# Token rows kept in PSUM through the expert blocks, and one weight load for the fullest expert's two blocks

## The reference, cut to what matters

```
gl = x2 @ w_rg + b_rg                        # 4 groups, the best is taken
el = x2 @ w_re + b_re                        # 8 experts in it, the best 2 are taken
w  = softmax(two logits) * p(group)
for each chosen (token, expert):             # 32 experts, 1024 -> 512 -> 1024
    y += w * ((silu(x @ w_gate[e]) * (x @ w_up[e])) @ w_down[e])
h  = h + y
out = rmsnorm(h) * final_norm_g
```

## Time and profile before

| | us |
|---|---|
| median of 3 runs (1507.97 to 1509.42) | 1508.8 |
| the profiled execution's own time | 1504.2 |
| its span, first to last instruction | 1502.6 |
| PE busy | 1150.9 (77%) |
| DVE busy | 464.5 (31%) |
| ACT busy | 234.5 (16%) |
| POOL busy | 207.2 (14%) |

### The profile page before, as it was taken

The page is one execution under the profiler, slowest core; times in us unless marked ns, Lnnn a source line. Parts: engine busy times, 40 slices in busy tenths (PEclk is TensorE's granted clock), DMA queues, the critical chain, the costliest instruction groups (busy, mean ns, idle before and its releaser), DMA issues. The chain is left out here.

```text
span 1502.6 us, 22749 instructions
## 1 busy us (share of the span) xinstructions
PE 1150.9 (77%) x7953; PEld 729.8 (49%) x7953; DVE 464.5 (31%) x1117; ACT 234.5 (16%) x646; POOL 207.2 (14%) x402
## 2 busy tenths in 40 slices
PE   5899999999995898877899999666565656565650
PEld 3666667666763455554566664443232333232320
DVE  2235654656455574333000001331111111111113
ACT  1132233223322353222000000000000000000000
POOL 3033433344324111010000000000000000000003
PEclk9799999999997998999899999678887888787875
DMA  6033424332422226542965360299999999999963
GB/s 197 20 113 88 115 84 143 104 99 84 143 59 56 51 49 175 133 148 84 255 155 134 80 232 0 77 413 426 429 428 428 428 427 429 429 427 428 428 283 123
DMA packets 171882, 315.69 MB, mean 210 GB/s; under 512 B 22162, under 2 KB 153810, under 8 KB 159170
## 3 DMA queue, kind: packets, MB, share of 16 engines
q1 hardware_dynamic: 161842, 303.34, 56.1%
q0 software_dynamic: 2048, 6.95, 1.6%
q10 hardware_dynamic: 7952, 4.88, 1.1%
HBM read 296.02 MB, written 19.11 MB: 210 GB/s over the span
## 5 line engine op out<-in xcount | busy, mean ns | idle before, releaser
L1696 PE MATMUL ph<-w_gate_up,x_gathered 128*32 128x256 f32 x1408 | 121.8, 521 | 108.7 <-DMA w_gate_up<-in_w_exp_up 108.1
L669 PE MATMUL psg<-stretch 128*128 128x336 f32 x512 | 159.8, 477 | 11.3 <-DVE h_sample_out L647 9.6
L1696 PEld LDWEIGHTS ph<-w_gate_up,x_gathered 128*32 128x32 f32 x1408 | 60.5, 148 | 170.1 <-issue 98.1
L669 PEld LDWEIGHTS psg<-stretch 128*128 128x128 f32 x512 | 103.7, 204 | 69.2 <-DVE h_sample_out L647 15.4
L1664 DVE SCALAR_TENSOR_TENSOR h_gate<-h_tanh,ph 128x128 f32<-128x128 f32 x33 | 9.5, 287 | 387.3 <-ACT h_tanh L1624 387.3
L1696 PE MATMUL ph<-stretch,x_gathered 128*32 128x256 f32 x704 | 60.7, 519 | 57.9 <-DMA stretch<-in_w_exp_up 57.9
L584 DVE SCALAR_TENSOR_TENSOR x_conv<-x_padded,conv_wh,x_conv 128x360 f32<-128x360 f32 x96 | 56.9, 593 | 101.0 <-ACT x_conv L533 90.0
L678 PE MATMUL psg<-stretch 128*128 128x256 f32 (+1 forms) x384 | 84.5, 380 | 0.0
L1346 PE MATMUL psm<-stretch,w_merge 128*128 128x336 f32 x256 | 75.8, 455 | 6.9 <-DMA w_merge<-in_w_in 6.9
L1745 POOL DMA_INDIRECT y_expert<-expert_rows,slot_i x6 | 5.7, 958 | 505.8 <-PEq L1715 504.2
L678 PEld LDWEIGHTS psg<-stretch 128*128 128x128 f32 (+1 forms) x384 | 67.3, 177 | 14.5
(11 more groups left out here) (415 smaller groups left out, 1659.4 us busy)
## 6 DMA issues: line engine op xcount, KB each, us to landing
w_down<-in_w_exp_down SPq DMA_DIRECT2D x33, 2048.0 KB, 40.4
w_gate_up<-in_w_exp_gate SPq DMA_DIRECT2D x22, 2048.0 KB, 33.8
w_gate_up<-in_w_exp_up SPq DMA_DIRECT2D x22, 2048.0 KB, 38.4
stretch<-in_w_exp_gate SPq DMA_DIRECT2D x11, 2048.0 KB, 34.1
stretch<-in_w_exp_up SPq DMA_DIRECT2D x11, 2048.0 KB, 38.7
stretch<-in_w_in SPq DMA_DIRECT2D x16, 1024.0 KB, 5.3
stretch<-in_w_in SPq DMA_DIRECT2D x16, 512.0 KB, 7.5
h<-in_state_ssm SPq DMA_DIRECT2D x16, 512.0 KB, 4.8
```

What stands on the lines that cost most here:

```text
L669: mm = pe.matmul(ps[m][:, 0:T], wg[:, k, P * m:P * m + P], S["xnT"][:, k, :], start=(k == 0), stop=(k == KT - 1))
L1696: mm = pe.matmul(ph[h][32 * j:32 * j + 32, 0:256], xg[h][:, k, :], w_gu[w][:, :, k, P * j:P * j + P], start=(k == 0), stop=(k == KT - 1))
```

## The change

- `xtok` is multiplied by the identity into six PSUM banks (`acc`) in the route phase, as the start of a sum that stays open. The six banks hold the 336 rows until the end; `ph`, `px` and `py` share the other two.
- The slots of the pairs and their weights are also laid out along the free axis on all partitions (`slot_row`, `weight_row`): 12 matmul calls, four ACT copies, two POOL and two DVE multiplications in the route phase.
- In each block DVE makes from them a matrix `back` (32 slots x 4 groups of partitions, 336 tokens: the weight where slot and token belong together; four more instructions). After `py` has been copied to `yr`, PE adds the block to `acc` by 12 calls. A call has 32 rows of `yr` (one group of partitions j, a quarter of the columns) against up to 128 tokens. DMAs to `ydram`, the buffer itself and its zeros are gone.
- The fullest expert (of 3 to 31) changes places with expert 28, so that it is block 28, and its rows 32 to 63 are block 31. Expert 31 is block 32. Block 31 loads nothing and uses the weights of block 28, which are still in buffer 1. Blocks over are counted from 33 (`NMAIN`) on. The expert of each block from 3 on is read from `blk_e`.
- `each_block`: a loop of 4 passes (blocks 0 to 23), blocks 24 to 32 written out, then the loop of 4 passes of six bodies under `If`. With the counts above all 24 of these are jumped over.
- The final phase is part of the moe phase: no gather and no sum, ACT squares `acc` once PE has closed it, and DVE scales from `acc` to `xtok`.

```diff
+NMAIN = NE + 1
+TWICE, AGAIN = 28, 31
-NBLK = NE + NOVER
+NBLK = NMAIN + NOVER
+ADD_ORDER = [(0, 0), (0, 1), (0, 2), (0, 3), (1, 0), (1, 1), (1, 2), (1, 3), (2, 0), (2, 2), (2, 1), (2, 3)]
@@ attention_phase
-            sp.dma_start(S["ydram"][NE * BLK:SLOTS, :].rearrange("(b p) d -> p b d", p=64),
...
-            v.memset(blank, 0.0)
@@ route_phase, gpsimd
+            pool.wait_ge(topw_ok, 1)
+            for j in range(2):
+                pool.tensor_tensor(dgw[:, j, :, :], bc(S["ident"][:, :].unsqueeze(1), [P, 3, P]),
+                                   bc(S["topw"][:, :, j:j + 1], [P, 3, P]), ALU.mult).then_inc(dgw_ok, 1)
@@ route_phase, scalar
+            for j in range(2):
+                act.wait_ge(row_ps, j + 1)
+                act.activation(S["slot_row"][:, j, :], ps[j][:, 128:128 + T], ACT.Copy).then_inc(row_ev, 1)
... (the same for weight_row)
@@ route_phase, tensor, ahead of and behind the nine matmuls
+            for j in range(4):
+                pe.matmul(acc[:, j, :], S["ident"][:, :], S["xtok"][:, 0:2, 256 * j:256 * j + 256],
+                          start=True, stop=False)
+            for i in range(2):
+                pe.matmul(acc[0:80, 4 + i, :], S["ident"][0:80, 0:80], S["xtok"][0:80, 2, 512 * i:512 * i + 512],
+                          start=True, stop=False)
...
+            for src, ok, freed in ((dgs, dgs_ok, 0), (dgw, dgw_ok, 2)):
+                for j in range(2):
+                    pe.wait_ge(ok, j + 1)
...
+                    for t, r in enumerate(ROWS):
+                        mm = pe.matmul(ps[j][:, 128 + COL[t]:128 + COL[t] + r], o[0:r, :], src[0:r, j, t, 0:r],
+                                       start=True, stop=True)
+                    mm.then_inc(row_ps, 1)
@@ route_phase, vector, behind the nine matmuls: 45 instructions in place of 23, from
+            v.scalar_tensor_tensor(key[:, :], cnt[:, :], 64.0, keyb[:, :], ALU.mult, ALU.add)
...
+            v.tensor_reduce(topn[:, 0:1], key[:, :], AX.X, ALU.max)
...
+            for j in range(2):
+                v.tensor_tensor(dgs[:, j, :, :], bc(S["ident"][:, :].unsqueeze(1), [P, 3, P]),
+                                bc(S["slot"][:, :, j:j + 1], [P, 3, P]), ALU.mult).then_inc(dgs_ok, 1)
@@ moe_phase, each_block
-            sure = NE // UNROLL
+            sure = TWICE // UNROLL
             with eng.Fori(0, sure) as i:
                 for u in range(UNROLL):
-                    body(UNROLL * i + u, u, i)
-            with eng.Fori(sure, -(-NBLK // UNROLL)) as i:
+                    body(UNROLL * i + u, u, 2 * i + loads(u))
+            for b in range(sure * UNROLL, NMAIN):
+                body(b, b, loads(b))
+            with eng.Fori(0, -(-NOVER // UNROLL)) as i:
                 for u in range(UNROLL):
-                    with eng.If(UNROLL * i + u < nblk):
-                        body(UNROLL * i + u, u, i)
+                    with eng.If(UNROLL * i + u + NMAIN < nblk):
+                        body(UNROLL * i + u + NMAIN, u + NMAIN, 2 * i + loads(u + NMAIN))
@@ moe_phase, sync
-            for b in range(3, NE):
+            with sp.Fori(1, 10) as i:
+                for u in range(3):
+                    load(3 * i + u, u, bass.ds(3 * i + u, 1))
+            for b in (30, 32):
+                load(b, b % 3, slice(b, b + 1))
@@ moe_phase, scalar
-                act.wait_ge(y_sent[h], 64 * (3 * i + u // 2) + 64)
-                act.activation(yr[h][:, :], py[h][:, 0:256], ACT.Copy).then_inc(y_ev, 1)
+                act.wait_ge(added, b + 1)
+                act.activation(yr[h][:, :], py[:, :], ACT.Copy).then_inc(y_ev, 1)
...
-                for j in range(4):
-                    act.dma_start(ydram[bass.ds(BLK * b, BLK), j, :], yr[h][32 * j:32 * j + 32, :]
...
+            act.wait_ge(all_added, 1)
+            for t in (2, 0, 1):
+                act.activation(as_tile(xsq[0:r, :], t), tile_rows(t), ACT.Square, ...
@@ moe_phase, vector
+            def weights_back(b, h):
+                v.scalar_tensor_tensor(weq[:, :, :], slot_row[:, :, :], lane[:, 0:1], weight_row[:, :, :],
+                                       ALU.is_equal, ALU.mult)
+                v.drain()
+                v.wait_ge(added, b + 1)
+                v.tensor_tensor(back[h][:, :], weq[:, 0, :], weq[:, 1, :], ALU.add).then_inc(back_ok, 1)
+                v.tensor_scalar(lane[:, :], lane[:, :], float(BLK), None, ALU.add)
@@ moe_phase, tensor, body: gate, up and gather as before, then
                 pe.wait_ge(ht_ok, b + 1)
+                pe.wait_ge(xt_ok, b + 2)
... (down)
+                pe.wait_ge(y_ev, b + 2)
+                pe.wait_ge(back_ok, b + 1)
+                for t, j in ADD_ORDER:
+                    r, q = ROWS[t], slice(32 * j, 32 * j + 32)
+                    if (t, j) == (2, 1):
+                        mm.then_inc(tail_half, 1)
+                        pe.wait_ge(tail_half, b + 1)
+                    mm = pe.matmul(token_rows(t, j), back[h][q, COL[t]:COL[t] + r], yr[h][q, :], start=False,
+                                   stop=False)
+                mm.then_inc(added, 1)
@@ moe_phase, tensor, at the end
+            for i in range(6):
+                r = P if i < 4 else 80
+                mm = pe.matmul(acc[0:r, i, 0:CLOSE], S["zeros"][:, 0:r], S["ident"][:, 0:CLOSE], start=False, stop=True)
+            mm.then_inc(all_added, 1)
-def final_phase(nc, A, S, sem):
...
```

More of the change, by code:

```diff
@@ L901, in _ @@
                     load_kv(2 * i + half, half, True)
-            sp.wait_ge(blank_out, 16)
         @block.gpsimd
@@ L1405, in route_phase @@
                                                                      "mask_ok", "rank_ps"))
+        topw_ok, dgw_ok, dgs_ok, row_ps, row_ev = (sem(n) for n in ("topw_ok", "weight_diag_ok", "slot_diag_ok",
+                                                                    "slot_row_ps", "slot_row_ev"))
+        acc = S["acc"]
         block = ctx.enter_context(nc.Block())
@@ L1515, in _ @@
+            v.tensor_copy(rank[0:80, 2, :], ps[0][0:80, 64:96])
+            v.drain()
+            v.tensor_scalar(most[:, :], key[:, :], topn[:, 0:1], None, ALU.is_equal)
+            v.tensor_reduce(nb[:, :], over[:, :, :], AX.X, ALU.add)
+            v.drain()
+            v.tensor_tensor(far2[:, :], most[:, :], over[:, :, 0], ALU.mult)
+            v.tensor_tensor(key[:, :], most[:, :], to28[:, :], ALU.mult)
             v.tensor_scalar(late[:, :, :], rank[:, :, :], BLK - 0.5, None, ALU.is_gt)
@@ L1575, in moe_phase @@
         yr = [tsb(f"y_block{h}", [P, 256]) for h in range(2)]
-        px, ph, py = ([ctx.enter_context(nc.psum_tensor(f"{n}{h}", [P, 512], F32)) for h in range(2)]
-                      for n in ("px", "ph", "py"))
+        lane, lane_b = tsb("lane", [P, 1]), tsb("lane_shift", [P, 4])
+        weq, back = tsb("weighted_eq", [P, 2, T]), [tsb(f"weights_back{h}", [P, T]) for h in range(2)]
+        fg, ss = tsb("final_g", [P, D]), tsb("ss3", [P, 4])
+        out = S["xtok"]
+        xsq = S["hn"][:, 0, :]
@@ L1671, in body @@
                 pick(h)
+                v.drain()
+                weights_back(b + 1, 1 - h)
             pick(0)
+            for j in range(3):
+                v.tensor_scalar(lane_b[:, j:j + 1], S["part_f"][:, 0:1], 32.0 * (j + 1) - 0.5, -float(BLK), ALU.is_gt,
+                                ALU.mult)
+            v.drain()
+            v.tensor_tensor(lane[:, :], lane_b[:, 0:1], lane_b[:, 1:2], ALU.add)
+            v.drain()
+            v.tensor_tensor(lane[:, :], lane[:, :], lane_b[:, 2:3], ALU.add)
+            v.drain()
+            v.tensor_tensor(lane[:, :], lane[:, :], S["part_f"][:, 0:1], ALU.add)
             gathered(1, 0)
             pick(1)
+            v.drain()
+            weights_back(0, 0)
             each_block(v, nblk, body)
+            v.wait_ge(g_in, 16)
+            for t, n in ((2, 1), (0, 3), (1, 3)):
+                r = ROWS[t]
+                v.wait_ge(ssq, 6 + n)
+                v.wait_ge(rs_ok, 6 + max(n - 1 + t % 2, 1))
+                v.scalar_tensor_tensor(as_tile(out[0:r, t, :], t), tile_rows(t), ss[0:r, t:t + 1],
+                                       as_tile(fg[0:r, :], t), ALU.mult, ALU.mult).then_inc(out_ok, 1)
         @block.tensor
```

262 lines of the change are left out of this document (142 added, 120 removed).

## The result

The changed kernel takes 1571.05 us (median of 4, 1568.52 to 1574.21), the kernel before 1508.38 (4 runs, 1506.86 to 1509.42): ratio 1.0417, 95% interval 1.0396 to 1.0439, so 4.2% slower. The profiled execution took 1570.66 with a span of 1569.0. The forecast was 1494.6. What came true is rival A (1561.6), and the time lies 5 us above the range.

What follows compares the result with a forecast made beforehand. It took moe to be bound by weight transfers (15.0 us an expert), with route, jumps and final uncovered. Terms -6.9 (up to the jumps), +11.9, -18.3, -0.9 sum to -14.2: 1494.6 us, own range 1484 to 1505, whole range 1485 to 1566.

Steps and rivals of the forecast that it cites:

- rival A: Loop of six bodies no longer stays in PE's instruction memory, later passes miss: +67 us, 1561.6; chance 0.35.
- The jumps: PE's jumps over never-run bodies after the last block: 27.5 us in place of 15.6, +12 us.
- B: Only the dropped instruction packet is fetched again, once a pass: +10.5 us, 1505; chance 0.10.
- The main loop: Loop over the main blocks: instruction misses there would lie hidden under the 14.7 us of a load.
- Route: Route phase before moe: more DVE instructions (+4.3) and slot and weight rows (+5.2), +9.5 us, bounds +8 and +15.
- D: Route costs more, ranks delayed and DVE at its old average: +5.5 us, 1500; chance 0.06.
- The stream: Weight transfers in moe: one load less (14.7 us) and no writes of `y` (10 us), -24.7 us.
- that hole: Start of moe, 998 to 1013 us: the DMA queue runs dry for a moment, 1.4 us lost.
- The last blocks: Blocks 30 to 32 run in a row on PE, block 32 starting 9.1 us after its weights: +8 us given back.
- C: Adds don't overlap between groups of partitions: 2.9 us more in each of the last three blocks, +9, 1503.5; chance 0.04.
- Final: From the closing matmuls to the end: 11.0 us in place of 29.3, gather and sum gone, -18.3 us.
- the attention term: Start of the attention phase, before route: DVE's memset of 0.91 us goes, -0.9 us.

Runs made afterwards that it cites:

- shift64: The changed kernel with 16 useless one-column matmuls (64 PE instructions) behind block 28, moving the loop over further blocks within its page: 1504.0 us, ratio 0.9960.
- straight: `guard` with the 33 main blocks written out one after the other on PE, ACT and DVE in place of a loop: 1474.7 us, ratio 0.9783.
- guard: The changed kernel with the whole loop over further blocks inside one If on every engine, one jump in place of 24: 1478.4 us, ratio 0.9802.
- early_pair: `straight` with the fullest expert's two blocks at 13 and 16 in place of 28 and 31: 1471.4 us, ratio 0.9751.
- reload: `guard` with a weight load put back for block 31 (expert 31's weights, as many bytes), undoing the saved load: 1485.6 us, ratio 0.9851.
- jump_hidden: `early_pair` with the jump over the further blocks ahead of block 32 instead of behind it: 1472.3 us, ratio 0.9759.
- short_bodies: The changed kernel with one add of twelve in the never-run bodies over, cutting that loop from 1797 to 1533 instructions: 1501.1 us, ratio 0.9950.

## Why the prediction was wrong, step by step

**The jumps** are the step that failed: "six jumps over bodies that never ran [...] and three passes of 2.65: 27.5". Measured 96.2, so 68.7 too little; rival A's term was 67. `shift64` shows the forecast's own number where the loop stays: its jumps last from 1463.4 to 1490.9, 27.5 us. So the step rested on one assumption, that the longer loop stays in PE's instruction memory, and the prediction gave it 0.45 against 0.35 with the count of pages (eight or nine) in hand and "that eight do is shown nowhere" written down. The Trainium skill ("Runtime: NRT & Kernel Launch", section "Instruction fetch mechanics") has the FIFO of 2048 instructions and the sequential fetch from which the ninth page follows; the ten loops and the nine packets a pass above agree with that part of the section, and this rule should have had the larger chance. Rival A was also put too simply: it "decides from the first packet too many", while with eight pages the place in the last page decides. Even a reader sure of A's mechanism would have needed the loop's address. B (one packet a pass) is excluded: nine packets came in a pass, and nearly every jump missed.

**The main loop:** "the same misses would lie under the 14.7 of a load" was right. Its branch back misses three times at 6.3 to 6.6 us, and writing the blocks out brought 3 to 4 us (`straight` against `guard`), which is within the intervals.

**Route:** +7.7 against +9.5. DVE's chain took 11.7 (982.45 to the end of 994.13), forecast 11.6. The multiplications into `acc` did delay the ranks (980.56 behind 978.84), but they took 0.30 to 0.39 a pair in place of 0.6, so they ended 10.0 after route's start and not 11.2. The granted clock over them was 1.00 (980.5 to 982.45 us), before 0.50 (975.8 to 979.5): the effect that the prediction named ("they may also bring PE to the high clock") and took as 0. The rows cost 5.4 behind the chain (to 999.49), forecast 5.2. D, with its +5.5 for route, is excluded.

**The stream:** -24.7 was too much, a term of the wrong size. In `early_pair`, where block 32 waits for its weights, it starts 430.0 after the first refill, against 450.1 before, so -20.1:

```profile
1013.43 0.34 SPq L1629 DMA_DIRECT2D w_gate_up<-in_w_exp_gate  x1
```

The queue of the weights in the window of 1100 to 1400 us, before and after:

```profile
q1 hardware_dynamic: 8636, 125.77, 98.2%
```

```profile
q1 hardware_dynamic: 8777, 127.78, 100.1%
```

The 428 and 427 GB/s of the windows hold all queues together, before with the writes of `y`. By the bytes of the weights alone a load of 6.29 MB went from 15.0 us to 14.77. So leaving out the writes gave 0.24 us a load in place of 0.35, some 3 us of the 4.6 over 29 loads. In the same window the instruction queue went from 1 packet to 27, 0.6% of the engines' time, which takes back a part; no run separates the two. The rest, nearly 2 us, lies at the start of the stream: in `early_pair` the engines had run dry before the first refill (5 GB/s from 1010 to 1013 us), before they had not (426 GB/s from 995 to 998). The prediction had that hole, 1.4 us, the same on both sides.

**The last blocks:** right. Block 31 starts 13.3 behind block 30 (forecast 13.6), block 32 10.3 behind block 31 (forecast 10.2), and block 32 starts 9.6 behind where 430.0 puts its weights (1440.7), forecast 9.1. `reload` shows the same from the other side. The adds take 2.29 (forecast 2.2): groups of partitions overlap, C is excluded. The sequencer came free for the jumps only with the last adds, 9.9 after the block's start in place of 8.0.

**Final:** 12.6 against 11.0. The closing matmuls took 2.40 in place of 0.5, at the low clock: in the hole before them it stood at 0.51, and in `guard`, where they take 2.40 too, it is 0.50 over them. In `jump_hidden`, at 1.00, they take 1.34, so the term was too small at either clock.

**To route:** +4.2 where -0.9 was forecast. The code up to there is the same apart from the zeros, and in the fourteen profiled executions of this case route's first load stands anywhere from 967.6 to 977.6, at 967.6, 968.2, 974.9, 977.5 and 977.6 in the five kernels whose code up to there is that of before. The profiled execution of before was at the low end, so the attention term (-0.9) can't be read from it. Why it varies stays open, and so does whether it varies with the program or with the execution: the 38 runs of the kernel before beside the experiments lie from 1503.6 to 1513.0.

**The rest of the sum.** Without the jumps, the stretches stand 5.1 (to route), -1.8, 5.1, 1.9 and 1.7 off the forecast, +12.0 together: a span of 1500.4 in place of 1488.4. `short_bodies` and `shift64`, where the jumps are as forecast, have spans of 1499.5 and 1503.6 and took 1501.1 and 1504.0, at the upper end of the forecast's own range (1484 to 1505). These 12 us, and not the jumps, put the measured time above rival A's 1561.6 too, and above the range; the 5.1 to route's start are the part without a known cause.

**The chances.** Those by sign (0.55, 0.07, 0.38) don't follow from those by rival. B's 1505 lies below the 1508.8 of before, so half of its 0.10 is "same" and the other half "faster": 0.60, 0.05 and 0.35.

## What to carry to other kernels

A body that is unrolled under a loop is paid for in instruction pages even where it never runs. Count the instructions of each loop on the busiest sequencer before adding to the body, keep the loop at seven pages or fewer (all such loops stayed here), and put one test around a loop that usually has nothing to do (here 92.7 us). Saving a transfer just ahead of the end gives back only what the engine behind it can catch up (7.4 us of 14.7 here, with an uncertainty of some 5).

## What the runs showed of the hardware that was not expected

- 64 instructions that do nothing changed the time of the same kernel by 67 us, by where a loop of 1797 instructions ended in a page (37.99 or 38.24).
- A loop that does not stay had nine pages fetched in each pass, though it lies on eight.
- A jump to code not at hand costs 2.8 to 3.8 us in most cases and 4.6 to 5.1 in some, every time in a loop that does not stay; a branch back 4.6 to 5.0 in the `If` loops and 6.3 to 6.6 in the main loop; one jump over some 1800 instructions took 3.3 to 3.7, one over 2094 took 6.4 where PE was at work on the block ahead of it. Why the last two are longer was not tried.
- Twelve adds of 256 columns on four groups of 32 partitions took 2.29 us in each block.
- Leaving out a queue that held 2.7% of the DMA engines' time sped up the weights by 1.6% (15.0 to 14.77 us a load), with 0.6% of that time now going to the fetching of code.
